# Clearing the modulation sums on another engine, and reordering VectorE's work around the first MLP and the second attention of a two-block transformer kernel

## The reference

```python
def ada_modulation(c, w, b):
    m = jax.nn.silu(c) @ w + b
    shift, scale, gate = jnp.split(m[:, None, :], 3, axis=-1)
    return shift, scale, 1.0 + gate

for layer in range(DEPTH):
    shift, scale, gate = ada_modulation(c, ada_w[layer, 0], ada_b[layer, 0])
    h = x * (1.0 + scale) + shift
    y = mixer_ab(h, ...) if layer % 2 == 0 else mixer_c(h, ...)   # two attentions
    x = layer_norm(DN_ALPHA * x + gate * y, ln_g[layer, 0], ln_b[layer, 0])
    shift, scale, gate = ada_modulation(c, ada_w[layer, 1], ada_b[layer, 1])
    h = x * (1.0 + scale) + shift
    y = squared_relu_mlp(h, mlp_w1[layer], mlp_w2[layer])
    x = layer_norm(DN_ALPHA * x + gate * y, ln_g[layer, 1], ln_b[layer, 1])
```

## Time and profile before

| | us |
|---|---|
| three timed runs: median (lowest to highest) | 1424.16 (1422.37 to 1427.53) |
| the profiled execution, its own time | 1425.12 |
| its span in the profile | 1423.3 |
| TensorE busy | 1327.8 (93%) |
| VectorE busy | 1009.4 (71%) |
| ScalarE busy | 594.0 (42%) |
| GpSimd busy | 13.1 (1%) |

### The profile page before, as it was taken

The page is one execution under the profiler, slowest core; times in us unless marked ns, Lnnn a source line. Parts: engine busy times, 40 slices in busy tenths (PEclk is TensorE's granted clock), DMA queues, the critical chain, the costliest instruction groups (busy, mean ns, idle before and its releaser), DMA issues.

```text
span 1423.3 us, 20748 instructions
## 1 busy us (share of the span) xinstructions
PE 1327.8 (93%) x7932; PEld 1122.1 (79%) x7932; DVE 1009.4 (71%) x1358; ACT 594.0 (42%) x803; POOL 13.1 (1%) x22
## 2 busy tenths in 40 slices
PE   5886989999989999999999988999999988999997
PEld 1763677888888878888889987888888877888886
DVE  2667478988788878776688884866668665566665
ACT  2433443434343534434454322543437553443432
POOL 0000000000000000000000000000000000000000
PEclk8997989999999998999999999999999999999999
DMA  9753437877457635765535430555553330455540
GB/s 384 279 208 118 149 119 297 306 296 295 162 195 268 196 119 189 261 221 217 204 113 208 149 119 1 207 191 195 200 182 124 115 147 31 165 217 195 199 154 30
DMA packets 45791, 264.18 MB, mean 186 GB/s; under 512 B 5399, under 2 KB 7063, under 8 KB 19994
## 3 DMA queue, kind: packets, MB, share of 16 engines
q1 hardware_dynamic: 32624, 218.19, 42.0%
q10 hardware_dynamic: 13102, 45.09, 9.1%
HBM read 260.89 MB, written 1.05 MB: 184 GB/s over the span
## 4 chain that ended last, share of the span: by engine, by line
PE 78%; DVE 11%; DMA 4%; ACT 4%; issue 2%; SPq 0%; POOL 0%; ACTq 0%; DVEq 0%; POOLq 0%
PE banks L572 15%; PE banks L573 15%; PE banks L574 15%; PE banks L920 14%; PE banks L923 7%; DMA A<-ada_w 2%; DVE w_lo L1835 2%; PE banks L1215 2%; DMA raw<-stream 1%; PE banks L802 1%; ACT w_hi L1257 1%; PE banks L784 1%; PE banks L749 1%; PE banks L870 1%; PE banks L815 1%
## 5 line engine op out<-in xcount | busy, mean ns | idle before, releaser
L1835 DVE TENSOR_TENSOR w_lo<-raw,w_hi 128x2048 fp32r<-128x2048 f32 x193 | 439.6, 2286 | 119.5 <-ACT w_hi L1257 116.2
L1257 ACT ACTIVATE w_hi<-raw 128x2048 fp32r<-128x2048 f32 x193 | 368.4, 1914 | 235.1 <-PE banks L574 205.6
L920 PE MATMUL banks<-hT,w_hi 128*128 128x512 f32 x896 | 280.8, 395 | 0.0
L572 PE MATMUL banks<-w_hi,R 128*128 128x512 f32 (+1 forms) x624 | 246.5, 395 | 7.6 <-DVE R L1815 3.6
L573 PE MATMUL banks<-w_lo,R 128*128 128x512 f32 (+1 forms) x624 | 243.8, 391 | 0.0
L574 PE MATMUL banks<-w_hi,R 128*128 128x512 f32 (+1 forms) x624 | 243.4, 390 | 0.0
L923 PEld LDWEIGHTS banks<-hT,w_lo 128*128 128x128 f32 x896 | 168.3, 188 | 39.2
L923 PE MATMUL banks<-hT,w_lo 128*128 128x256 f32 x896 | 176.0, 278 | 0.0
L572 PE MATMUL banks<-hT,w_hi 128*128 128x256 f32 x536 | 158.4, 296 | 7.6 <-DVE hT L2307 5.6
L573 PE MATMUL banks<-hT,w_hi 128*128 128x256 f32 x536 | 153.9, 287 | 0.0
L574 PE MATMUL banks<-hT,w_lo 128*128 128x256 f32 x536 | 153.8, 287 | 0.0
(11 more groups left out here) (266 smaller groups left out, 1495.4 us busy)
## 6 DMA issues: line engine op xcount, KB each, us to landing
raw<-stream SPq DMA_DIRECT2D x193, 1024.0 KB, 4.8
A<-ada_w ACTq DMA_DIRECT2D x73, 512.0 KB, 5.4
A<-ada_w SPq DMA_DIRECT2D x6, 1024.0 KB, 16.7
raw<-ada_w SPq DMA_DIRECT2D x3, 1024.0 KB, 7.2
A<-ln_g ACTq DMA_DIRECT2D x4, 512.0 KB, 3.7
A<-ln_b ACTq DMA_DIRECT2D x4, 512.0 KB, 5.5
A<-ada_w SPq DMA_DIRECT2D x1, 1536.0 KB
A<-A SPq DMA_DIRECT2D x20, 64.0 KB, 4.0
```

What stands on the lines that cost most here:

```text
L572: pe.matmul(o, lh, rh, start=start, stop=False, skip_group_check=True)
L920: pe.matmul(two(B[2 * kp + a]), wh[:, kt, P * a:P * a + P], hT[:, :, kt, :], start=kt == 0, stop=False, skip_group_check=True)
L1257: act.activation(w_hi[:, s, :], raw[:, s, :], ACT.Copy).then_inc(hi_done, 1)
L1835: v.tensor_tensor(w_lo[:, s, :], raw[:, s, :], w_hi[:, s, :], ALU.subtract).then_inc(lo_done, 1)
```

## The change

- The clear of `ada_acc` moves from VectorE (`zero_acc`) to GpSimd, in both places. For MLP 0 GpSimd waits only for `col_ready` 2 (the columns of modulation 1 are made); in the second attention it waits for TensorE's gate matmul, as VectorE did.
- In MLP 0, VectorE waits for the bias behind the three `low`, not ahead of them.
- In the second attention the step `("gate", 2)` stands behind the read of CU's result.
- In round 2 of the second attention `rope(1)` stands ahead of `rest`, so ahead of the `low` of CU+9. Round 1 has no modulation sum, and round 4 has two.

```diff
@@ c_steps @@
                 s += fills(CU + j, "N", "h", "plain", [arena(C_V, TT, D)[:, :, 256 * j:256 * j + 256]])
+                if j == 0:
+                    s += [("gate", 2)]
...
-                s += (exps(c) if c >= 0 else []) + fills(u, "T", "h", "rope", [C_TMP]) + rest(u - 1 + SLOTS)
+                s += (exps(c) if c >= 0 else []) + fills(u, "T", "h", "rope", [C_TMP])
+                s += rope(1) if j == 2 else []
+                s += rest(u - 1 + SLOTS)
                 s += (spread(c) if c >= 0 else []) + [("ahead", u)]
-                if j:
+                if j and j != 2:
                     s += rope(j - 1)
-                s += some(1)
+                s += some({1: 0, 4: 2}.get(j, 1))
...
-        STEPS += bound(1, "ln", M0 + 31, mod, lead=(CU, CU + 1)) + [("gate", 2)] + c_steps()
+        STEPS += bound(1, "ln", M0 + 31, mod, lead=(CU, CU + 1)) + c_steps()
@@ gpsimd @@
-                if kind == "norm2":
+                if kind == "gate":
+                    g.wait_ge(gate_ps, a[0] + 1)
+                    g.memset(ada_acc, 0.0).then_inc(acc_zero, 1)
+                elif kind == "mlp" and a[2]:
+                    g.wait_ge(col_ready, 2)
+                    g.memset(ada_acc, 0.0).then_inc(acc_zero, 1)
+                elif kind == "norm2":
@@ vector, mlp @@
-                if s_ada:
-                    zero_acc()
-                    v.wait_ge(ld_bias, 16 * (s_ada + 1))
                 for u in range(u0, u0 + 3):
                     low_ahead(u)
+                if s_ada:
+                    v.wait_ge(ld_bias, 16 * (s_ada + 1))
@@ vector, steps @@
-                elif kind in ("gate", "gate0"):
-                    if kind == "gate":
-                        v.wait_ge(gate_ps, a[0] + 1)
-                        zero_acc()
```

More of the change, by code:

```diff
@@ L1994, in bend @@
                     v.tensor_scalar(k, f, -1.0, 1.0, ALU.mult, ALU.add).then_inc(silu_done, 1)
-            def zero_acc():
-                v.memset(ada_acc, 0.0).then_inc(acc_zero, 1)
             v.memset(zero8[:, :], 0.0)
```

## The result

| | before | changed |
|---|---|---|
| median of 13 runs of each (lowest to highest), us | 1423.85 (1418.42 to 1427.81) | 1430.45 (1426.98 to 1433.35) |
| profiled execution, us | 1425.12 | 1431.42 |
| its span, us | 1423.3 | 1429.6 |
| mean granted clock of TensorE | 0.972 | 0.967 |

The ratio is 1.005, with an interval of 1.0036 to 1.0063: the change made the kernel slower by 0.5%, 6.6 us between the medians. The kernel before was some 2 us faster in the rounds of the experiments than in this one, so the changed kernel is set beside an experiment by the ratios. Predicted were 1418.9, with 1425.5 as the upper end.

The account below looks back on a forecast made before the run. The chain is 78% TensorE, so its gaps at the edited places count. Terms 3.4 - 2.35 + 4.2 = 5.2 us gained take 1425.12 to 1419.9; the median, 1.0 lower, is 1418.9, range 1414.5 to 1425.5.

Parts of the forecast that it names:

- part 1: Start of MLP 0: `low` earlier, down 1 without a gap, down 2 at 235.3 instead of 238.73; 3.4 us gained.
- the hold: GpSimd's clear ahead of MLP 0 keeps the shared ports and may hold VectorE's `half` for 2.35 us.
- transfers ran in the order of issue: Start of MLP 0: loads move in issue order, not sharing bandwidth; carried the second `late` landing at 231.4.
- Rival (b): MLP 0: `late` loads share bandwidth with stream units, second lands at 235.6, down 2 starts at 239.5; 1424.8 us, chance 0.08.
- Part 2: GpSimd's clear ahead of MLP 0 takes 2.7 us and may hold `half`, on the chain, for 2.35 us.
- (a): Ahead of MLP 0, GpSimd's clear doesn't hold VectorE; 7.6 us gained, 1416.6 us, chance 0.27.
- (c): Ahead of MLP 0, GpSimd's clear is long and holds `half` throughout; a 12 us clear gives 1428.2 us, chance 0.10.
- Part 3: Second attention's gate step: ScalarE reads CU's result before the gate copies, TensorE's gap at 409.56 goes; 1.84 us gained.
- Part 4: Second attention's rotation: scores 3.6 us earlier, 1.84 of it the gate step's, 1.2 for the clock, 0.6 off; 4.2 gained.
- rival (d): Second attention gains only its 1.84, as VectorE waits for the sums' loads either way; 2.9 gained, 1421.3 us, chance 0.15.
- down 2 waiting over 2.5 us: Sign in MLP 0 that the prediction is wrong; the forecast had down 2 waiting 1 to 2 us for the square.

Follow-up runs that it names:

- e4: e3 with VectorE's bias wait put back ahead of the three `low` in MLP 0; 1421.49 us, ratio 1.0 to the kernel before.
- e5: e3 with MLP 0's gate-sum loads issued ahead of the modulation loads, modulation bias wait behind the `late` sums; 1417.31 us, ratio 0.9978 to the kernel before.
- the five: Five profiled executions with MLP 0 as in the kernel before; their MLP 0 took 187.3 to 189.9 us, mean 188.3.
- e3: Changed kernel with GpSimd's clear for MLP 0 waiting until VectorE has done the `low` of M0+1; 1429.39 us, ratio 1.005 to the kernel before.
- e7: Kernel before with only the second attention's gate step moved and its clear on GpSimd; 1421.78 us, ratio 1.001.
- e2: Kernel before with only the change's second-attention part, MLP 0 as before; 1419.13 us, ratio 0.9981.
- e6: e2 with the modulation sums' first two loads issued in the second attention's gate step; 1417.29 us, ratio 0.9963 to the kernel before.
- e11: Kernel before with only MLP 0's loads reordered, gate-sum loads ahead of the modulation bias and loads; 1431.13 us, ratio 1.0057.
- e9: Changed kernel, early clear kept, with MLP 0's gate-sum loads first and modulation bias wait behind the `late` sums; 1420.93 us, ratio 0.9987 to the kernel before.

## Why the prediction was wrong

**The step that failed** is in part 1: the landing of the second `late` load, put at 231.4, between 230.1 and 232.6. It landed at 238.3, 6.9 us later. 1.0 of that is its issue, which came 1.0 us earlier than before and not 2.0, as the hold had made ScalarE's list late. The rest is the sharing. Under the forecast lay the sentence "transfers ran in the order of issue". Read from one window, it was wrong. In the changed kernel q1's first load is issued at 220.49, ahead of both `late` loads, and its first packets move at about 224.8; from 226 on both queues move alike, packet for packet. In e4, issued at 225.80, q1 starts at about 228.6. In the kernel before it starts at about 228.6 too, 2.6 us behind the issue at 226.00; I looked at the first 2 us only and saw the lag. There q10 was nearly through by then (21 packets from 229 to 230), so that window could tell neither order from lag nor lag from sharing. The Trainium skill (DMA: Bandwidth & Descriptors, Queues, rings and completion order) says that each DMA engine takes turns between the queues, a packet at a time; by the equal counts the trace agrees, against what I wrote.

**Rival (b)** had the mechanism, with a chance of 0.08. Its landing of 235.6 was 2.7 early, and that is why down 2 starts at 242.37, and not at 239.5; the path from the second landing to down 2 took 4.1 us, near the 3.9 it used. The slow clock that it charged with 1.7 cost 2.4: down 2 takes 7.84 us to up 4's first matmul, where it took 5.45. In the sum: counted from bound 0's last `root`, down 2 starts 3.9 later than before, the hold among it, and 2.4 for the slow matmuls behind it make the 6.2 that MLP 0 lost. Rival (b) with its hold had 4.85.

**The rest of part 1** came as written: the `low` at 218.03, the bias landed behind their cover, down 1 without a gap. e5 seems to show what it was worth with down 2 on time: MLP 0 takes 184.6 us, 3.7 less than the mean of the five, beside the 2.8 + 1.7 of the prediction.

**Part 2** was right in mechanism and near in size: the clear took 2.65 us (2.7 forecast, with some luck, from two clears of 1 and 8 columns that differ by 6 ns), and `half` took 1.9 longer (2.35 forecast). The clear started 0.48 ahead of `half`, not 0.35, and `half` ended 0.28 behind it, not its whole 0.55. Its price on the chain was less: up 0 started at 199.90 instead of 198.21, but up 2 ended only 0.7 later, at 223.79 instead of 223.13, as the clock rose at about 203 in both. e3's ratio shows no gain from taking the hold away. Rivals (a) and (c) fall. The Trainium skill (SBUF — State Buffer, Who interferes with whom) has this as an exclusive lock; the rows agree, also for a `half` with two columns as operands. The 2.6 cycles an element of the Trainium skill (GPSIMD Engine Reference, Performance versus the Vector engine), which the section gives for an addition of two tensors, do not hold for a clear: 3072 columns in 2.65 us are 0.86 ns each.

**Part 3** had the right gap and the wrong consequence: the 1.84 us went, but the next thing late was the sums' load, and e7 gained nothing. **Part 4** gained 1.4 of 3.6 at the scores in the changed kernel, 2.3 in e2, and in the changed kernel the 1.2 for the clock didn't come (1.65 us for the first eight matmuls). This has rival (d)'s cause, VectorE's waits for the sums' loads: 10.3 us from bound 1's last `root` to the first scores in the changed kernel, 8.8 in e2, 6.0 before. How much of the loss they make isn't shown, since e6 takes away only part of them.

The sum was thus 6.2 us lost in MLP 0 where 1.05 (3.4 - 2.35) was to be gained, and in the attention 0.4 (the changed kernel's profile) to 2.6 (e2's median) gained instead of 4.2. Of the signs that the prediction named for being wrong, "down 2 waiting over 2.5 us" is the one that came.

## What to carry to other kernels

A wait that looks idle may be what keeps two groups of transfers apart: before moving it, list which buffers the work behind it frees, which loads that starts, and which load of another queue is then due. Here the two queues shared the DMA engines by packets, so the loads with short rows lost against those with long rows; put the load that stands in front of TensorE first in its queue (in e5 a `late` load, in the order of e11 still the bias). And when work is taken off an engine that waits for transfers, look first at whether the transfer comes earlier, or only the waiting gets longer.

## What the runs showed of the hardware

A queue whose load was issued while another kept the engines busy moved its first packets 2.6 to 4.3 us later (226.00 to 228.6 in the kernel before, 220.49 to 224.8 in the changed one); in e11, where the other queue was just running out, it was 0.8 (229.96 to 230.8). What sets this time isn't shown. Once it ran, both got the same number of packets and not the same bytes: 0.30 MB of 8 KB rows and 0.12 MB of 4 KB rows in one microsecond. GpSimd's clear of 128x3072 takes 2.65 us, as VectorE's did (2.63), and a VectorE instruction of one source that started 0.48 us behind it ended 0.28 us behind its end, after 2.45 us instead of 0.55. The first three `low` of MLP 0, which have two sources, took 6.69 us with the clear beside them (e3) and 6.69 without (e9).
